# The second MLP of a float32 two-block network in pairs of column chunks, some of its units with seven block products in place of eight

## What is computed

```python
h2 = _rms_norm(x, norm2_g[l])
x = x + (jax.nn.silu(h2 @ w_gate[l]) * (h2 @ w_up[l])) @ w_down[l]
```

## Time and profile before

| | |
|---|---|
| median of 3 runs | 2490.76 us (2490.45 to 2491.49) |
| the profiled execution, its own time | 2491.81 us |
| its span, first to last instruction | 2490.1 us |
| TensorE busy with matmuls | 2479.4 us |
| VectorE busy | 1379.7 us |
| ScalarE busy | 1120.4 us |

### The profile page before, as it was taken

One profiled execution on the slowest core, in us unless ns is written; L12 is line 12 of the kernel. 1 busy time (PEld: TensorE's weight loads), 2 busy tenths in 40 slices (PEclk: granted clock), 3 DMA queues, 4 the chain that ended last, 5 costly groups with the idle time before them and its releaser, 6 DMA issues.

```text
span 2490.1 us, 27992 instructions
## 1 busy us (share of the span) xinstructions
PE 2479.4 (100%) x11851; PEld 2073.6 (83%) x11851; DVE 1379.7 (55%) x1130; ACT 1120.4 (45%) x1100; POOL 116.4 (5%) x95
## 2 busy tenths in 40 slices
PE   9999999999999999999999999999999999999999
PEld 7888888888888888888888888788888888888887
DVE  5775455454655555545555568876544444444444
ACT  5545533334444434334434458874533333333332
POOL 0410010010100000000000010000200000000000
PEclk9999999999999999999999999999999999999999
DMA  7555465656656555555555555444555655565554
GB/s 250 174 181 185 154 202 186 202 187 199 223 189 204 194 191 186 197 191 186 195 191 188 186 186 186 138 160 160 186 186 186 198 191 186 187 200 187 187 190 147
DMA packets 243306, 467.11 MB, mean 188 GB/s; under 512 B 11312, under 2 KB 23104, under 8 KB 242798
## 3 DMA queue, kind: packets, MB, share of 16 engines
q1 hardware_dynamic: 241630, 460.08, 56.8%
q10 hardware_dynamic: 1552, 5.25, 0.6%
HBM read 463.20 MB, written 2.10 MB: 187 GB/s over the span
## 4 chain that ended last, share of the span: by engine, by line
PE 97%; DVE 1%; ACT 1%; issue 0%; DMA 0%; POOL 0%; SPq 0%; DVEq 0%; ACTq 0%; POOLq 0%
PE acc L423 26%; PE acc L414 26%; PE acc L416 26%; PE acc L443 5%; PE acc L449 2%; PE tp L443 2%; PE sd L443 2%; PE sd L449 1%; PE tp L449 1%; PE tp L469 1%; PE sd L1377 1%; PE tp L1395 0%; DVE wlo L399 0%; PE sd L1386 0%; ACT whi L391 0%
## 5 line engine op out<-in xcount | busy, mean ns | idle before, releaser
L399 DVE TENSOR_TENSOR wlo<-raw,whi 128x2048 fp32r<-128x2048 f32 (+1 forms) x440 | 1014.0, 2306 | 955.7 <-ACT whi L391 955.0
L391 ACT ACTIVATE whi<-raw 128x2048 fp32r<-128x2048 f32 (+1 forms) x440 | 832.3, 1893 | 1068.7 <-PE acc L423 920.3
L414 PE MATMUL acc<-whi,opA_hi 128*128 128x512 f32 x1888 | 741.1, 393 | 0.0
L416 PE MATMUL acc<-whi,opA_lo 128*128 128x512 f32 x1888 | 735.4, 390 | 0.0
L423 PE MATMUL acc<-wlo,opA_hi 128*128 128x512 f32 x1888 | 469.2, 390 | 0.2 <-DVE wlo L399 0.2
L414 PE MATMUL acc<-whi,opB 128*128 128x512 f32 (+1 forms) x1088 | 422.3, 389 | 1.5 <-ACT whi L391 1.5
L416 PE MATMUL acc<-whi,opB 128*128 128x512 f32 (+1 forms) x1088 | 419.0, 386 | 0.0
L414 PEld LDWEIGHTS acc<-whi,opA_hi 128*128 128x128 f32 x1888 | 354.8, 188 | 73.9 <-issue 0.9
L416 PEld LDWEIGHTS acc<-whi,opA_lo 128*128 128x128 f32 x1888 | 354.8, 188 | 72.6
L423 PEld LDWEIGHTS acc<-wlo,opA_hi 128*128 128x128 f32 x1888 | 353.0, 188 | 73.4 <-DVE wlo L399 0.8
L423 PE MATMUL acc<-wlo,opB 128*128 128x512 f32 (+1 forms) x1088 | 266.4, 387 | 0.1
(11 more groups left out here) (307 smaller groups left out, 1286.8 us busy)
## 6 DMA issues: line engine op xcount, KB each, us to landing
raw<-in_w_in SPq DMA_DIRECT2D x114, 1024.0 KB, 5.5
raw<-in_w_mlp_up SPq DMA_DIRECT2D x64, 1024.0 KB, 5.5
raw<-in_w_mlp_down SPq DMA_DIRECT2D x64, 1024.0 KB, 5.0
raw<-in_w_gate SPq DMA_DIRECT2D x44, 1024.0 KB, 5.1
raw<-in_w_up SPq DMA_DIRECT2D x44, 1024.0 KB, 5.2
raw<-in_w_down SPq DMA_DIRECT2D x44, 1024.0 KB, 5.0
raw<-in_w_out SPq DMA_DIRECT2D x32, 1024.0 KB, 5.0
raw<-in_w_branch SPq DMA_DIRECT2D x16, 1024.0 KB, 5.0
```

The source lines that it names most:

```text
L391: eng.activation(whi[:, j % SPL, k, 0:cols], raw[:, j, k, 0:cols], ACT.Copy).then_inc(hi_split, share(k))
L399: eng.tensor_tensor(wlo[:, j % SPL, k, 0:cols], raw[:, j, k, 0:cols], whi[:, j % SPL, k, 0:cols].bitcast(F32), ALU.subtract).then_inc(lo_s ...
L414: eng.matmul(acc[:, pair, m, 0:cols], hi[:, kt + i, m * P:(m + 1) * P], whi[:, s, i, 0:cols], start=first and i == 0, stop=False)
L416: eng.matmul(acc[:, pair, m, 0:cols], lo[:, kt + i, m * P:(m + 1) * P], whi[:, s, i, 0:cols], start=False, stop=False)
```

## The change

**Pairs.** The 132 units keep their number and bytes, but hold other tiles: two row tiles of two column chunks (`raw` is seen as tile 2a+b: row tile a, chunk b), loaded by two DMAs of 0.5 MB instead of one of 1 MB. A gate pair is 8 units that fill all four banks at once: chunk c of `w_gate` in `acc[:, 0, m]` and of `w_up` in `acc[:, 1, m]`. A down pair is two column chunks of `w_down` (6 units in the first part, 8 in the other two). There are 11 gate pairs and 6 down pairs, in the order 3 gate, 2 down, 4 gate, 2 down, 4 gate, 2 down (`PAIRS`, numbered 0 to 16). A pair's first and last units go bank by bank (`plain_products`), so that banks are asked for and finished one after another; each bank waits for the unit's low part after four matmuls.

**Seven products.** Units 3 and 5 of a pair (`GATE_SEVEN`, `DOWN_SEVEN`; only unit 5 in pair 0, unit 3 in pair 3, units 1 and 3 in pair 4) are a 2 x 2 by 2 x 2 block product done with seven block products instead of eight (the scheme of Strassen and Winograd), so 21 matmuls in place of 24. VectorE makes four sums of weight tiles (`t_sum`), ScalarE and VectorE split three tiles and these four (`seven_hi`, `seven_lo`, buffers of their own), and VectorE makes four sums of activation blocks once for each place (`operand_sums`, `operand_low`; eight times in all, kept for all pairs of the same kind). The products go into the four banks, and three sums into `sd` and `tp`. In all 32 units are of this kind: 21 in gate pairs, 11 in down pairs.

**Putting together.** Behind the low part of a pair's last unit VectorE runs `combine`, with the sums of `sd` and `tp`; for a down pair also three additions to `xres`. `finish_first` then adds to the pair's first bank, ahead of the low part of the next pair's first unit; `finish` does the other banks behind it.

The core of the diff:

```diff
+GATE_SEVEN, DOWN_SEVEN = (3, 5), (3, 5)
...
+                PAIRS.append(Pair(len(PAIRS), "gate", unit, PAIR_UNITS, GATE_SEVEN if PAIRS else GATE_SEVEN[1:], 0,
+                                  GATE_SEVEN, (part, c), chunks2))
...
+                seven = DOWN_SEVEN if part else (1, 3) if n else (3,)
...
+        A_SUMS = {(0, 1): (0, GATE_SEVEN[0], 0), (0, 2): (0, GATE_SEVEN[1], 1)}
+        for q in PAIRS:
+            if q.kind == "gate" and PAIRS[q.n + 1].kind == "down":
+                A_SUMS[q.n, 1] = (1, PAIRS[q.n + 1].places[0], 0)
+                A_SUMS[q.n + 1, 1] = (1, PAIRS[q.n + 1].places[1], 1)
...
-                    load_unit(sp, G_PAIR0 + 2 * CH2_FIRST + u // UN, u % UN, w_dn2, UK * k, n * NW)
...
+                    sp.wait_ge(lo_split, (u - RAW + 1) * HV)
+                    to = raw[:, u % RAW].rearrange("p (a b) c -> p a b c", a=2)
+                    for b in range(2):
+                        if p.kind == "gate":
+                            src = (w_gate2, w_up2)[b][:, 2 * v:2 * v + 2, chunk(first + n)]
+                        else:
+                            src = w_dn2[:, first * CT + 2 * v:first * CT + 2 * v + 2, chunk(2 * n + b)]
+                        sp.dma_start(to[:, :, b, :], src).then_inc(landed[u % RAW], 16)
...
+            def seven_high(p, v):
+
+                u, n = p.unit + v, sevens_before(p, v)
+                act.wait_ge(landed[u % RAW], loads_before(u // UN + 1) * 16)
+                if last_seven(p, v):
+                    act.wait_ge(units_used, last_seven(p, v))
+                act.activation(seven_hi[:, 0, :], raw[:, u % RAW, 0, :], ACT.Copy)
+                act.activation(seven_hi[:, 1:3, :], raw[:, u % RAW, 2:4, :], ACT.Copy).then_inc(hi_split, 1)
+                act.wait_ge(t_made, 3 * n + 1)
+                act.activation(seven_hi[:, 3:5, :], t_sum[:, 0:2, :], ACT.Copy)
+                act.wait_ge(t_made, 3 * n + 3)
+                act.activation(seven_hi[:, 5:7, :], t_sum[:, 2:4, :], ACT.Copy).then_inc(hi_split, 1)
...
+                    if (p.n, v) in A_SUMS:
+                        k, _, x = A_SUMS[p.n, v]
+                        act.wait_ge(a_made, list(A_SUMS).index((p.n, v)) + 1)
+                        act.activation(a_hi[k][:, x, :, :], a_sum[:, :, :], ACT.Copy).then_inc(a_high, 1)
...
+                    if v == p.units - 1:
+                        act.wait_ge(units_used, p.unit + p.seven[-1] + 1)
...
+                        act.activation(q_sum[:, :], sd[:, 0, :], ACT.Copy).then_inc(q_copied, 1)
...
+            def bank_free(p, b, m):
+
+                if p.n == 0:
+                    pe.wait_ge(read_dve, readers_before(R_PAIR0 - 1 + b, "D") * MT)
+                elif PAIRS[p.n - 1].kind == "gate" and b == 0:
+                    pe.wait_ge(silu_in, PAIRS[p.n - 1].gates * MT + m + 1)
+                else:
+                    pe.wait_ge(bank_read, 4 * (p.n - 1) + 2 * b + m + 1)
...
+                banks = [(b, m) for b in range(2) for m in range(MT)]
+                if first or last:
+                    for b, m in banks:
+                        if first:
+                            bank_free(p, b, m)
+                        for a in range(2):
+                            high(b, m, a)
+                        pe.wait_ge(lo_split, (u + 1) * HV)
+                        for a in range(2):
+                            mm = low(b, m, a)
+                        if last and (b, m) != banks[-1]:
+                            mm.then_inc(bank_done, 1)
...
+                own = [(sd[:, 0, :], (hi[:, k1, up], lo[:, k1, up]), 0, True),
+                       (acc[:, 0, 0, :], (hi[:, k2, up], lo[:, k2, up]), 1, False),
+                       (acc[:, 1, 0, :], sums(0), 2, False)]
+                made = [(sd[:, 1, :], sums(1), 3, True), (tp[:, 1, :], sums(2), 4, True), (tp[:, 0, :], sums(3), 5, True),
+                        (acc[:, 0, 1, :], (hi[:, k2, down], lo[:, k2, down]), 6, False)]
...
+                pe.wait_ge(a_low, sums_made(p, v))
+                for done, products in ((1, own), (2, made)):
+                    pe.wait_ge(hi_split, u * HV + done)
+                    for bank, (a_h, a_l), i, alone in products:
+                        pe.matmul(bank, a_h, seven_hi[:, i, :], start=alone and first, stop=False)
+                        pe.matmul(bank, a_l, seven_hi[:, i, :], start=False, stop=False)
+                    pe.wait_ge(lo_split, u * HV + done)
+                    for bank, (a_h, a_l), i, alone in products:
+                        mm = pe.matmul(bank, a_h, seven_lo[:, i, :], start=False, stop=alone and last)
+                mm.then_inc(units_used, 1)
...
+                dve.wait_ge(a_low, sums_made(p, v))
+
+                dve.tensor_tensor(t_sum[:, 0:2, :], w[:, 0:4:3, :], w[:, 1:2, :].to_broadcast([P, 2, NW]),
+                                  ALU.add).then_inc(t_made, 1)
+                dve.wait_ge(t_made, 3 * n + 1)
+                dve.tensor_tensor(t_sum[:, 2, :], t_sum[:, 0, :], w[:, 3, :], ALU.add).then_inc(t_made, 1)
+                dve.wait_ge(t_made, 3 * n + 2)
+                dve.tensor_tensor(t_sum[:, 3, :], t_sum[:, 2, :], w[:, 2, :], ALU.add).then_inc(t_made, 1)
+                if last_seven(p, v):
+                    dve.wait_ge(units_used, last_seven(p, v))
+                dve.wait_ge(hi_split, u * HV + 1)
+                dve.tensor_tensor(seven_lo[:, 0, :], w[:, 0, :], seven_hi[:, 0, :].bitcast(F32), ALU.subtract)
+                dve.tensor_tensor(seven_lo[:, 1:3, :], w[:, 2:4, :], seven_hi[:, 1:3, :].bitcast(F32),
+                                  ALU.subtract).then_inc(lo_split, 1)
+                dve.wait_ge(hi_split, u * HV + 2)
+                dve.wait_ge(t_made, 3 * n + 3)
+                dve.tensor_tensor(seven_lo[:, 3:7, :], t_sum[:, :, :], seven_hi[:, 3:7, :].bitcast(F32),
+                                  ALU.subtract).then_inc(lo_split, 1)
...
+                own.done(dve.tensor_tensor(a_full[:, :, :], hi[:, kt, :].bitcast(F32), lo[:, kt, :].bitcast(F32), ALU.add))
+                a11, a21, a12, a22 = [a_full[:, r, m * P:(m + 1) * P] for r in range(2) for m in range(MT)]
+                own.mark(dve.tensor_tensor(a_sum[:, 1, :], a21, a22, ALU.subtract))
+                own.done(dve.tensor_tensor(a_sum[:, 2, :], a21, a11, ALU.subtract))
+                own.done(dve.tensor_tensor(a_sum[:, 3, :], a22, a_sum[:, 2, :], ALU.subtract))
+                dve.tensor_tensor(a_sum[:, 0, :], a12, a_sum[:, 3, :], ALU.subtract).then_inc(a_made, 1)
...
+                dve.wait_ge(units_used, p.unit + p.seven[-1] + 1)
+                n = p.combined
+                dve.wait_ge(q_copied, p.n + 1)
+                if p.n:
+                    dve.wait_ge(combined, n)
+                    dve.wait_ge(bank_read, 4 * p.n)
+                dve.tensor_tensor(vw[:, 0, :], tp[:, 0, :], q_sum[:, :], ALU.subtract).then_inc(combined, 1)
+                dve.wait_ge(combined, n + 1)
+                dve.tensor_tensor(vw[:, 1, :], tp[:, 1, :], vw[:, 0, :], ALU.add).then_inc(combined, 1)
+                dve.wait_ge(combined, n + 2)
+                dve.tensor_tensor(yz[:, :, :], vw[:, :, :], sd[:, 1:2, :].to_broadcast([P, 2, NW]), ALU.add).then_inc(combined, 1)
+                if p.kind == "down":
+                    n1, n2 = chunk(2 * p.chunk[1]), chunk(2 * p.chunk[1] + 1)
+                    dve.tensor_tensor(xres[:, 0, n1], xres[:, 0, n1], q_sum[:, :], ALU.add).then_inc(combined, 1)
+                    own.mark(dve.tensor_tensor(xres[:, 1, n1], xres[:, 1, n1], vw[:, 1, :], ALU.subtract))
+                    dve.wait_ge(combined, n + 3)
+                    p.mark = own.mark(dve.tensor_tensor(xres[:, :, n2], xres[:, :, n2], yz[:, :, :], ALU.add))
...
+            def finish_first(p):
+
+                if p.kind == "down":
+                    dve.wait_ge(combined, p.combined + 4)
+                    own.need(p.mark)
+                    bank_to_x(p, 0, 0)
+                else:
+
+                    bank_wait(p, 0, 0)
+                    dve.tensor_tensor(acc[:, 0, 0, :], acc[:, 0, 0, :], q_sum[:, :], ALU.add).then_inc(bank_read, 1)
...
+                bank_wait(p, 0, 1)
+                dve.tensor_tensor(acc[:, 0, 1, :], acc[:, 0, 1, :], vw[:, 1, :], ALU.subtract).then_inc(bank_read, 1)
+                dve.wait_ge(combined, p.combined + 3)
                 for m in range(MT):
-                    dve.scalar_tensor_tensor(stage[:, m, :], acc[:, run % 2, m, :], rstd[:, m:m + 1], silu_gate[:, m, :],
-                                             ALU.mult, ALU.mult).then_inc(read_dve, 1)
...
+                    bank_wait(p, 1, m)
+                    dve.tensor_tensor(stage[:, m, :], acc[:, 1, m, :], yz[:, m, :], ALU.add).then_inc(bank_read, 1)
+                    dve.wait_ge(bank_read, 4 * p.n + 2 + m + 1)
+                    dve.wait_ge(silu_in, p.gates * MT + m + 1)
```

(40 more changed lines are left out.)

278 lines of the change are left out of this document (150 added, 128 removed).

## The result

The changed kernel takes 2476.74 us, median of 4 runs (2475.95 to 2476.94), against 2491.12 us of the kernel before (2490.45 to 2491.78, with a fourth run beside the three of the table of the kernel before): 14.4 us less, a ratio of 0.9942 (95% interval 0.9926 to 0.9958). The prediction was 2477.4 us, from the median of three runs. The profiled execution took 2476.92 us by its own time, its span is 2475.2 us, 14.9 under the span before.

What follows compares the result with a forecast made beforehand. TensorE was taken as the bound, by number and spacing of matmuls. The sum -21.7 + 5.8 + 0.3 + 2.3 = -13.3 us turned 2490.8 into 2477.4 us, range 2470.5 to 2485.5.

Steps and rivals of the forecast that it cites:

- 96 matmuls fewer: Second MLP: 32 units need only 21 matmuls each in place of 24, at 0.2265 us per matmul: 21.7 us gained.
- five places behind down pairs: Before the next pair, TensorE waits 1.0 us for the low part and 0.15 for the second bank: 5.8 us in all.
- pair 4's second unit: TensorE asks for this unit's seven-product low parts before VectorE has them: 0.3 us lost, once.
- first pair, unit 3: Operand sums and their copies delay ScalarE's high part for this unit; TensorE waits 2.3 us, bounds nothing to 3.
- gate pairs, seven-product units, loads, end: No wait between gate pairs, at seven-product units or for loads, and nothing gained or lost at the end: 0 us.
- the stretch: Second MLP, from its first matmul to the last: all gains and losses together make it 13.3 us shorter.
- The spacing: Six matmuls in one bank in a row keep the 0.227 us rhythm; the page's 131 ns was not used.
- The 0.15 for the second bank: Behind down pairs, TensorE waits 0.15 us more because VectorE reads the second bank too late.
- its lower bound: Behind down pairs, if dependent VectorE instructions cost no more than free ones, the five places cost 2 us.
- The covers of the seven-product units: Low parts ready ahead of TensorE by 0.2 to 0.3 us with operand sums, 1.9 without, 1.5 at unit 5.
- the rival in which these units give back what they save: Every seven-product unit waits 0.3 to 0.5 us for its own low parts: 2487 to 2493 us, chance 0.10.
- VectorE as the bound: Rival: seven-product chains outgrow their covers, as with repeated, strided operands at half rate; up to 2525 us, chance 0.06.

Runs made afterwards that it cites:

- e10: The change with additions to `xres` moved behind the next pair's second low part, TensorE not waiting for them, plus the move of e2: 2469.48 us.
- e2: The change with ScalarE's copy of the operand sums (`a_sum`) put one unit later, behind the next high part: 2474.49 us.
- e4: The change with one seven-product unit in a pair and two in pair 4, 18 in place of 32: 2485.97 us.
- e7: The change with two more instructions of 512 columns in `combine` of each gate pair, more work for VectorE: 2484.17 us.

## Why the prediction held, and where its steps were off

| step | predicted us | measured us |
|---|---|---|
| 96 matmuls fewer | -21.7 | -21.8 (e10 against before) |
| five places behind down pairs | +5.8 | +5.4 |
| pair 4's second unit | +0.3 | 0 |
| first pair, unit 3 | +2.3 | +1.9 |
| gate pairs, seven-product units, loads, end | 0 | 0; some +0.2 in starts late by under 0.1 each |
| the stretch | -13.3 | -14.3 |

**The spacing.** Six matmuls in one bank in a row keep the same 0.2265 us. By the Trainium skill's figure for pairs of weight load and matmul (TensorE: Matmul & The Clock Gate, Back-to-back issue gap) the 96 would have been worth an estimated 12.6 us. e10 shows 21.8, so the row was the one to go by.

**Behind down pairs** the mechanism was right, and the mis-sized term is the one from the earlier trace rows: that an instruction that depends on the one before it costs its length plus 0.11. The rows after give 2163.72 - 2163.00 = 0.72 for 512 columns, the length 0.69 plus 0.03; 1.26 from end to end for L2458 (1.22 long), where I had 1.33; and 1.31 from L2464 (1.22 long) to L2475. The chain begins where I had it, and the low part ends 0.20 sooner (1.62 on the prediction's scale, not 1.82); the handover takes 0.05 (2170.99 to 2171.04) and not 0.1. So the wait for the low part is 0.76 and not 1.0. The 0.15 for the second bank came as predicted. Against the 0.25 too much stands what I had not counted: a matmul behind a wait is followed by one that is 0.11 late. That the two partly cancel, and 1.15 comes as near as it does to 1.02, is luck. The page from which the prediction took its lower bound (the Trainium skill, VectorE: DVE Perf Modes, The DRAIN you can't avoid) tells of eight copies that take the same time with a semaphore behind each; the bound read from it, that dependence costs nothing, is not what these rows of additions show: independent neighbours start 0.60 apart (2165.59 to 2166.19), dependent ones 0.72. Why has 0.80 was not tried.

**The first pair** came as it was followed, behind the copies of `a_sum`, and e2 shows the cause. Each set of sums took 1.85 us, not 2.02 (1761.82 to 1763.67), and two such sets make up 0.34 of the 0.5 by which the wait itself is shorter (1.76 in place of 2.3); the 0.11 on the next matmul was not counted.

**The covers of the seven-product units** were the weak term. I had 0.2 to 0.3 us where operand sums are made. Pair 3's unit 3, with operand sums, in the timeline after:

```profile
1904.85 1.22 DVE L2411 TENSOR_TENSOR seven_lo<-raw,seven_hi 128x1024 fp32r<-128x1024 f32 x1
...
1906.92 0.39 PE L1841 MATMUL sd<-seven_lo,opA_hi 128*128 128x512 f32 x1
```

The unit's own low parts are done at 1906.07 and asked for at 1906.92, 0.85 to spare. Elsewhere it is 1.1 with operand sums and 2.5 to 3.3 without; only pair 4 has less, 0.11 at its second unit and 1.66 at its fourth. The trace of pair 8, on the prediction's scale, shows where the difference arises: the other banks are done and multiplied at 2.53 and not 2.8, the operand sums end at 6.52 and not 7.05, the sums `t_sum` at 15.77 and not 16.55, and the unit's own low parts at 17.52 and not 18.3. Each of these stretches holds additions that depend on the one before, which I had taken too long. So the rival in which these units give back what they save was farther off than its 0.10.

**VectorE as the bound** fell with the operation it rested on. Groups of VectorE in the second MLP (busy us, mean ns):

```profile
L2401 DVE TENSOR_TENSOR t_sum<-raw 128x1024 f32<-128x1024 f32 x32 | 39.0, 1218 | 0.1
...
L2406 DVE TENSOR_TENSOR t_sum<-t_sum,raw 128x512 f32<-128x512 f32 x32 | 22.1, 692 | 1.1
```

L2401 reads one tile twice, as a repeated operand, and tiles 0 and 3 as the other. Neither cost anything extra: 1218 ns for 1024 columns, as the earlier trace rows have for a plain one.

**Open.** The first place behind a down pair (pair 3 to 4) waits 0.28 us more than the others, and not in e4, whose pairs 3 and 4 have the same seven-product units. In the change ScalarE starts the high part of pair 3's last unit at 1910.89, 0.80 behind the last matmul of the seven-product unit ahead of it; elsewhere it is about 0.51. e2 and e7 have both as well (0.80, and 1.06 and 1.04 in place of 0.76), while in e4 ScalarE starts 0.51 behind. That it is this 0.3 that arrives is argued from the times. What delays ScalarE there was not found; the weights, which landed by 1898.3, are not it.
